# Two expert weight tiles per layer beside the ring, and a first pass of the expert loop written out

## The reference

```python
x += mixer(rmsnorm(x))        # layer 0: dilated sliding-window attention, layer 1: latent attention
x += hier_moe(rmsnorm(x))
x += (p[i] @ W_ple) * sigmoid(rmsnorm(x) @ W_ple_gate)
```

## Time and profile before

| | us |
|---|---|
| median of 3 runs | 1383.76 |
| lowest, highest | 1382.33, 1385.93 |
| profiled execution | 1388.38 |
| its span, first to last instruction | 1386.5 |

### The profile page before, as it was taken

How to read it: one execution, slowest core, us unless ns; L and a number is a source line. 1 busy time by engine, 2 the same in 40 slices (tenths; PEclk the granted TensorE clock), 3 DMA queues, 4 the chain that set the end, 5 groups by cost and what they waited for, 6 DMA issues and landing times.

```text
span 1386.5 us, 31096 instructions
## 1 busy us (share of the span) xinstructions
PE 1059.5 (76%) x13804; PEld 824.0 (59%) x13804; DVE 455.1 (33%) x1019; ACT 294.6 (21%) x567; POOL 9.3 (1%) x19
## 2 busy tenths in 40 slices
PE   6999999988666666666667989986666766765667
PEld 6999999865444545453445756564454444544446
DVE  6545555552112111111113675521121211111127
ACT  5433444221000000000003654210000000000017
POOL 1000000000000000000000000000000000000000
PEclk9999999999787998988898999998887888789888
DMA  9986540689999999999999740499999999999980
GB/s 275 313 235 173 159 123 0 260 370 425 426 426 426 426 426 426 425 427 425 426 427 385 307 173 1 182 428 425 429 424 426 428 424 426 428 423 425 427 347 32
DMA packets 114671, 470.02 MB, mean 339 GB/s; under 512 B 4689, under 2 KB 79569, under 8 KB 89841
## 3 DMA queue, kind: packets, MB, share of 16 engines
q1 hardware_dynamic: 113856, 465.78, 83.9%
q0 software_dynamic: 688, 2.28, 0.4%
HBM read 467.00 MB, written 1.05 MB: 338 GB/s over the span
## 4 chain that ended last, share of the span: by engine, by line
DMA 51%; PE 42%; DVE 3%; issue 2%; ACT 2%; DVEq 0%; SPq 0%; ACTq 0%
DMA ring<-moe_w_down 29%; DMA ring<-moe_w_up 11%; DMA ring<-moe_w_gate 11%; PE ps L1697 6%; PE ps L1468 5%; PE ps L1469 5%; PE ps L1470 5%; PE ps L1712 4%; PE ps L1582 2%; PE ps L1742 2%; PE ps L1784 1%; PE ps L1532 1%; PE ps L1508 1%; PE ps L1603 1%; PE ps L1875 1%
## 5 line engine op out<-in xcount | busy, mean ns | idle before, releaser
L1697 PE MATMUL ps<-ring,scr 128*32 128x128 f32 x8192 | 285.9, 300 | 154.3 <-DMA ring<-moe_w_up 98.7
L1697 PEld LDWEIGHTS ps<-ring,scr 128*32 128x32 f32 x8192 | 249.5, 120 | 192.8 <-DMA ring<-moe_w_up 109.2
L1712 PE MATMUL ps<-ring,scr 128*32 128x256 f32 x2048 | 175.3, 497 | 119.5 <-DMA ring<-moe_w_down 104.3
L1712 PEld LDWEIGHTS ps<-ring,scr 128*32 128x32 f32 x2048 | 83.8, 136 | 190.1 <-issue 118.4
L1188 DVE TENSOR_TENSOR scr<-scr,ps 128x128 f32<-128x128 f32 x64 | 23.8, 371 | 435.3 <-PE ps L1697 435.3
L728 ACT COPY scr<-ps 32x256 f32<-32x256 f32 x128 | 46.6, 364 | 552.7 <-PE ps L1712 551.9
L1201 DVE COPY scr<-ps 32x256 f32<-32x256 f32 x128 | 53.3, 417 | 248.7 <-PE ps L1712 247.8
L1468 PE MATMUL ps<-hT_hi,w_qk_hi 128*128 128x256 f32 x368 | 104.4, 284 | 0.0
L1470 PE MATMUL ps<-hT_hi,w_qk_lo 128*128 128x256 f32 x368 | 103.7, 282 | 0.0
L1469 PE MATMUL ps<-hT_lo,w_qk_hi 128*128 128x256 f32 x368 | 103.6, 282 | 0.0
L1603 PEld LDWEIGHTS ps<-scr,hs 128*128 128x128 f32 x512 | 66.3, 210 | 19.2 <-issue 19.2
(11 more groups left out here) (258 smaller groups left out, 1186.7 us busy)
## 6 DMA issues: line engine op xcount, KB each, us to landing
ring<-moe_w_gate SPq DMA_DIRECT2D x64, 2048.0 KB, 36.2
ring<-moe_w_up SPq DMA_DIRECT2D x64, 2048.0 KB, 36.6
ring<-moe_w_down SPq DMA_DIRECT2D x64, 2048.0 KB, 36.5
ring<-dsa_w_in SPq DMA_DIRECT2D x72, 512.0 KB, 6.7
ring<-ple_w_gate SPq DMA_DIRECT2D x4, 2048.0 KB, 37.0
ring<-dsa_w_out SPq DMA_DIRECT2D x2, 2048.0 KB, 13.9
ring<-mla_w_out SPq DMA_DIRECT2D x2, 2048.0 KB, 21.7
x_sb<-ple_w SPq DMA_DIRECT2D x2, 1024.0 KB, 7.1
```

What stands on the lines that cost most here:

```text
L1697: mm = pe.matmul(bank(b)[CW * q:CW * q + CW, 0:P], xT[:, k, :], tile(t + j, KD, FF)[:, k, P * q:P * q + P], start=(k == 0), stop=(k == KD ...
L1712: mm = pe.matmul(bank(6)[CW * q:CW * q + CW, 0:T], e_hT[:, CW * j:CW * j + CW], tile(t + 2, FF // P, D)[:, j, T * q:T * q + T], start=(j = ...
```

## The change

For each layer the down matrices of expert 0 and expert 1 (tiles 2 and 5 of the layer's order, `ASIDE`) leave the ring's numbering. They are kept in scratch, each in three pieces: two of its four row blocks together (1024 KB), and the other two alone (512 KB each), at places where `e_xT[1]` with `e_y`, `p_w`, `e_oneh` with what follows it, `f_gain` and `e_wt` will be later. SP issues three of the six pieces when the attention's last output product is done (`o_ready` in layer 0, `m_o_ready` in layer 1), before the ring tile that waits for the third `mix_out`, and the other three after the fourth `mix_out`. The eight tiles ahead of `ple_w` are then those numbered 0, 1, 3, 4, 6, 7, 8 and 9, and the loop on SP begins at tile 14. In layer 1 `f_gain` is loaded only after the second expert's down product, because its place holds a piece. The junk outputs of the squares get one buffer for both chunks, with a wait for the engine's own first square. On PE the first of the four passes is written out by a helper `expert(it, i)` with constants, whose down product for the first two experts reads the pieces, and the loop has three passes.

```diff
+ASIDE = (2, 5)
+SETTLED = RING + 6
+LOOPED = SETTLED + 3 * BODY * (ITERS - 1)
...
-    PLE = [MOE[0] + 3 * NE, 0]
+    PLE = [MOE[0] + 3 * NE - len(ASIDE), 0]
...
+        aside = [[scratch(3328, 2, D), scratch(9224, 1, D), scratch(10248, 1, D)],
+                 [scratch(256, 2, D), scratch(11272, 1, D), scratch(6528, 1, D)]]
...
-        junk_d, junk_a = [scratch(1024 * c, 512) for c in range(TC)], [scratch(1024 * c + 512, 512) for c in range(TC)]
+        junk_d, junk_a = scratch(2304, 512), scratch(2816, 512)
...
+            def load_aside(l, a, piece, rows):
+
+                e = ASIDE[a] // 3
+                sp.dma_start(aside[a][piece], moe_w_down[l, e:e + 1, :, :].rearrange("e (p j) n -> p (e j) n", p=P)[:, rows, :]
+                             ).then_inc(S(f"aside_{a}_in"), 16)
+
             def load_experts(l):
-                for n in range(RING):
+                ring_first = [n for n in range(SETTLED) if n not in ASIDE]
+                early, late = ring_first[:4 if l == 0 else 6], ring_first[4 if l == 0 else 6:RING]
+                for n in early:
+                    load_expert_tile(l, n)
+                if l == 0:
+                    sp.wait_ge(S("o_ready"), HEADS)
+                else:
+                    sp.wait_ge(S("m_o_ready"), MH // 2)
+                load_aside(l, 0, 0, slice(0, 2))
+                load_aside(l, 1, 0, slice(0, 2))
+                if l == 0:
+                    load_aside(l, 0, 1, slice(2, 3))
+                else:
+                    load_aside(l, 1, 2, slice(3, 4))
+                load_expert_tile(l, late[0])
+                sp.wait_ge(S("mix_out"), 4 * (l + 1))
+                if l == 1:
+                    load_aside(l, 0, 1, slice(2, 3))
+                load_aside(l, 0, 2, slice(3, 4))
+                load_expert_tile(l, late[1])
+                load_aside(l, 1, 1, slice(2, 3))
+                if l == 0:
+                    load_aside(l, 1, 2, slice(3, 4))
+                for n in late[2:]:
                     load_expert_tile(l, n)
 
                 sp.wait_ge(S("scattered"), (NGRP + 1) * l + 1)
                 sp.dma_start(x_sb[:, :, :], ple_w[l].rearrange("(k p) n -> p k n", p=P)).then_inc(S("p_in"), 16)
+                for n in ring_first[RING:]:
+                    load_expert_tile(l, n)
                 with sp.Fori(0, ITERS - 1) as it:
-                    for n in range(RING, RING + 3 * BODY):
+                    for n in range(SETTLED, SETTLED + 3 * BODY):
                         load_expert_tile(l, n, it)
...
                 if l == 1:
+                    pool.wait_ge(S("down_ready"), NE + ASIDE[1] // 3 + 1)
                     pool.dma_start(f_gain, rows[0:1, 2 * NR:2 * NR + D].partition_broadcast(P)
...
+                if i in (0, 1, 4) and c > 0:
+                    dve.wait_ge(S("sq_d"), TC * i + c)
...
-                with pe.Fori(0, ITERS) as it:
...
+                def wait_weights(it, i, j):
+
+                    if isinstance(it, int):
+                        t = Tiles.expert(l, 3 * i + j)
+                        wait_tile(pe, t)
+                    else:
+                        t = Tiles.expert(l, 3 * BODY + 3 * i + j)
+                        wait_tile(pe, t, (3 * BODY // RING) * (it - 1))
+                    return t
...
+                    if first and 3 * i + 2 in ASIDE:
+                        a = ASIDE.index(3 * i + 2)
+                        pe.wait_ge(S(f"aside_{a}_in"), 48 * (l + 1))
+                        down = [aside[a][0][:, 0, :], aside[a][0][:, 1, :], aside[a][1][:, 0, :], aside[a][2][:, 0, :]]
+                    else:
+                        t = wait_weights(it, i, 2)
+                        down = [tile(t, FF // P, D)[:, j, :] for j in range(FF // P)]
...
+                for i in range(BODY):
+                    expert(0, i)
+                with pe.Fori(1, ITERS) as it:
                     for i in range(BODY):
...
+                        expert(it, i)
```

More of the change, by code:

```diff
@@ L88, with expert, number @@
     MOE[1] = MLA_OUT + 2
-    PLE[1] = MOE[1] + 3 * NE
+    PLE[1] = MOE[1] + 3 * NE - len(ASIDE)
     N = PLE[1] + 2
+    @staticmethod
+    def expert(l, n):
+        assert n not in ASIDE
+        return Tiles.MOE[l] + n - sum(a < n for a in ASIDE)
+    @staticmethod
+    def number(l, t):
+        n = t - Tiles.MOE[l]
+        for a in ASIDE:
+            n += a <= n
+        return n
     @staticmethod
@@ L122, in used @@
         if t < Tiles.PLE[l]:
-            n = t - Tiles.MOE[l]
+            n = Tiles.number(l, t)
             return ("gate_ready", "up_ready", "down_ready")[n % 3], NE * l + n // 3 + 1
@@ L461, in load_expert_tile @@
             def load_expert_tile(l, n, it=0):
-                t, j = Tiles.MOE[l] + n, n % 3
+                t, j = Tiles.expert(l, n), n % 3
                 wait_free(t, BODY * it)
@@ new lines, in wait_weights, with expert @@
+                def wait_weights(it, i, j):
[6 more added lines that the diff above has]
+                    return t
+                def expert(it, i):
+                    first = isinstance(it, int)
+                    e = NE * l + BODY * it + i
+                    grp = (BODY // GE) * it + i // GE
+                    xT = e_xT[(i // GE) % 2][:, :, CW * (i % GE):CW * (i % GE) + CW]
+                    if i % GE == 0:
+                        pe.wait_ge(S("xT_ready"), xt0 + 2 * grp + 2)
+                    for j, b in ((0, 4), (1, 5)):
+                        t = wait_weights(it, i, j)
+                        for k in range(KD):
+                            for q in range(4):
+                                mm = pe.matmul(bank(b)[CW * q:CW * q + CW, 0:P], xT[:, k, :],
+                                               tile(t, KD, FF)[:, k, P * q:P * q + P],
+                                               start=(k == 0), stop=(k == KD - 1))
+                        mm.then_inc(S("gate_ready" if j == 0 else "up_ready"), 1)
+                    if i % GE == GE - 1:
+                        pe.wait_ge(S("wt_ready"), NGRP * l + grp + 1)
+                        pe.wait_ge(S("xT_ready"), xt0 + 2 * grp + 4)
+                        for c in range(TC):
+                            mm = pe.transpose(bank(7)[:, c * P:(c + 1) * P], e_wt[0][:, c, :], ident)
+                        mm.then_inc(S("wt_turned"), 1)
+                    pe.wait_ge(S("hT_ready_e"), e + 1)
+                    if first and 3 * i + 2 in ASIDE:
[5 more added lines that the diff above has]
+                        down = [tile(t, FF // P, D)[:, j, :] for j in range(FF // P)]
+                    for j in range(FF // P):
+                        for q in range(4):
+                            mm = pe.matmul(bank(6)[CW * q:CW * q + CW, 0:T], e_hT[:, CW * j:CW * j + CW],
+                                           down[j][:, T * q:T * q + T],
+                                           start=(j == 0), stop=(j == FF // P - 1))
+                    mm.then_inc(S("down_ready"), 1)
+                    if i == 1:
+                        pe.wait_ge(S("flag_ready"), l + 1)
+                    if i == GE:
+                        pe.wait_ge(S("pT_in"), 16 * (l + 1))
+                        pe.wait_ge(S("p_in"), 16 * (l + 1))
+                        for c in range(TC):
+                            for k in range(PLE // P):
+                                mm = pe.matmul(bank(7)[:, T * c:T * c + T], e_pT[:, k, c * P:(c + 1) * P],
+                                               x_sb[:, k, bass.ds(T * it, T)], start=(k == 0),
+                                               stop=(k == PLE // P - 1))
+                        mm.then_inc(S("pw_ready"), 1)
+                    if i == GE + 1:
+                        pe.wait_ge(S("pw_copied"), ITERS * l + it + 1)
+                    if i % GE in (1, 2):
+                        pe.wait_ge(S("oneh_ready"), TC * (NGRP * l + grp + 1))
+                        pe.wait_ge(S("xT_ready"), xt0 + 2 * grp + 2 + (i % GE - 1))
+                        gather(l, grp + 1, i % GE - 1)
+                    pe.wait_ge(S("y_copied_d"), e + 1)
+                    pe.wait_ge(S("y_copied_a"), e + 1)
+                    if i % GE == GE - 1:
+                        pe.wait_ge(S("sc_ready"), NGRP * l + grp + 1)
+                        for c in range(TC):
+                            for n in range(2):
+                                mm = pe.matmul(bank(2 * c + n), e_sc[:, c * P:(c + 1) * P],
+                                               e_y[:, 512 * n:512 * n + 512], start=False, stop=True,
+                                               skip_group_check=True)
+                            mm.then_inc(S("scattered" if c == TC - 1 else "scattered_0"), 1)
```

65 lines of the change are left out of this document (5 added, 60 removed).

## The result

The changed kernel takes 1366.63 us (median of 4 runs, 1364.75 to 1367.59). The kernel before, on the same chip, takes 1383.05 (4 runs). The ratio is 0.9864, 95% [0.9841, 0.9886]: on the 1383.76 of the prediction that is 18.8 us gained, between 15.8 and 22.0. The forecast was 14.6 gained, so 1369.2, with the range 1366.5 to 1373; the ratio puts the kernel at 1364.9, a little under the range. The two medians of this chip differ by less, 16.4 us, and the interval holds both; the same pair, timed again on another chip in experiment 6, gave 0.9868.

The account below looks back on a forecast made before the run. The prediction took DMA of expert weights at 425 GB/s to bound both loops. Layer 0's 6.0 us and layer 1's 8.6 made 14.6 gained, off the median 1383.76: 1369.2, own range 1366.5 to 1373, widened to 1366 to 1376.

Parts of the forecast that it names:

- the first pass written out: PE's expert loop, one jump back fewer per layer: value 0, bounds 5.75 us gained and up to 2.5 lost per written pass.
- it shifts whole: Between the expert loops and after the second, the change touches nothing on the chain, so no time is gained or lost.
- What bounds the kernel: Both expert loops: DMA of weight tiles at 425 GB/s sets the end; PE's pace inside the loop costs nothing.
- Layer 0's term: Layer 0's expert stream: 6.17 us gained by early pieces less 0.2 for short rows, 6.0 us in all.
- 6.17 us of stream are gained: Layer 0: three early pieces, 2.62 MB, fit into idle DMA time before the sixth tile, with about 1 us to spare.
- The term for short rows: Layer 0's pieces come in 8 and 4 KB rows, not 16 KB: 0.2 us lost, bounds 0 and 0.4.
- Layer 1's term: Layer 1's expert stream: 9.87 us gained by all six pieces less 1.3 for the later `f_gain`, 8.6 us in all.
- The same 152 us: Sign: the stretch from layer 0's last tile to layer 1's `ple_w` keeps its length of 152 us.
- rival (a): Half the gain: layer 1's routing slowed beside transfers, layer 0 possibly clipped; 6 to 8 us left, 1376.5; chance 0.12.
- (b): PE's code waits at the loops' pass changes are on the path: 14.6 + 11.5 us gained, 1357.7; chance 0.04.
- (d): Pieces don't queue into one another, 4.9 us each in the DMA queue: 10.4 us slower, 1394.2; chance 0.05.
- (c): Gain given back whole because PE, not DMA, ends the expert loop: 1383.8; chance 0.03.

Follow-up runs that it names:

- experiment 6: The changed kernel, unchanged, timed again on another chip: 1367.44 us, ratio 0.9868 to the kernel before.
- experiment 7: The changed kernel with the `f_gain` broadcast done four times, one after the other: 1372.42 us, ratio 0.9886 to the kernel before.
- experiment 1: The kernel before with only PE's first pass written out, no tiles beside the ring: 1379.82 us, ratio 0.9944.
- experiment 10: The changed kernel with both PE loop heads set at instruction 29 of a 16 KB code piece: 1367.74 us, ratio 0.986 to the kernel before.
- experiment 3: The changed kernel with PE's loop heads set at instructions 57 and 77 of a 16 KB code piece: 1372.1 us, ratio 0.9907 to the kernel before.
- experiment 2: The kernel before with 170 semaphore increments on PE around the first transposes of `x`, shifting later code: 1392.53 us, ratio 1.0058.
- 12: The kernel before, unchanged, run once more for a second profile: 1386.35 us, ratio 0.9995.
- experiment 9: The changed kernel with each piece beside the ring loaded by four issues in 1 KB rows: 1367.79 us, ratio 0.9862 to the kernel before.
- experiments 4: The changed kernel with tiles beside the ring in layer 1 alone: 1371.07 us, ratio 0.9889 to the kernel before.
- experiment 5: The changed kernel with tiles beside the ring in layer 0 alone: 1376.13 us, ratio 0.9921 to the kernel before.

## Why the prediction was wrong, and what of it held

The terms of the two tiles held. What failed is the step that put everything outside the two streams at nothing: the first pass written out at "Value 0", and "Between the loops and after the second nothing in the change touches the chain [...], so it shifts whole". Written out alone, the pass measured 7.7 us. With the routing that is told below, 14.0 of stream + 7.7 − 1.6 = 20.1, inside the measured 15.8 to 22.0.

**What bounds the kernel** held. The plateaus stay at 425 to 426 GB/s in every kernel of the study, and layers without the tiles take 491.9 to 494.1 and 445.1 to 446.1 us, with them 487.1 to 488.5 and 436.3 to 437.1 (the four `f_gain` of experiment 7 left out). The means of the two sets are 4.9 and 9.1 apart, 14.0 against 14.6 forecast.

**Layer 0's term** was 6.0 and is 4.9 (4.6 in the first pair of traces). The step that mis-sized it is "6.17 us of stream are gained": it asked whether the bytes fit and never summed the hole. In 4 us windows from 272 to 296, what lacks to 425 GB/s is 2.1, 0.4 and 3.2 us and, from a later look at the same trace, 1.3 and then nothing, about 7.0 in all. After it is 0.1, 0.1, 0.0, 1.2, 0.2 and 0.4, about 2.0. The gain is the difference, 5.0. The hole from 284 to 288, while the sixth tile's queue starts, is in both kernels. The term for short rows, 0.2, doesn't look like what is missing: with rows of 1 KB the stream is as long. The mean hides one more thing. Routing of layer 0 comes in a short and a long form (last section), and without the tiles the long one leaves a hole of its own: in experiment 1 the stream has 305 and 379 GB/s from 300 to 308, where before has 408 and 428. The streams without tiles are 491.9 to 492.2 with the short form and 493.4 and 494.1 with the long one; with tiles they are 487.1 to 488.5 with either. So the tiles are worth 4.5 or 5.9 in layer 0, by the form.

**Layer 1's term** was 8.6, with 1.3 off for `f_gain`; the stream gave 9.1 (9.6 in the first pair of traces). The pieces fit as forecast and no large hole opened behind `ple_w`. The three extra `f_gain` at 1.2 each confirm the price of an added one, the 0.2 for taking the only one away does not; both cannot be the whole story, and this stays open.

**The first pass written out, at value 0,** was wrong: 7.7 us, [0.9925, 0.9964]. The argument looked at the pass changes inside the loop, which indeed stay free. After, PE still waits 2.83 and 4.85 us at one of layer 1 and 3.02 us in the next expert, in a full stream:

```profile
1093.18 0.66 PE L1763 MATMUL ps<-ring,scr 128*32 128x128 f32 x8 [2.83 <-issue]
1098.69 5.69 PE L1763 MATMUL ps<-ring,scr 128*32 128x128 f32 x120 [4.85 <-issue]
...
1114.42 1.86 PE L1763 MATMUL ps<-ring,scr 128*32 128x128 f32 x26 [3.02 <-issue]
```

The upper bound, 5.75 for a pass change in each layer, was on the wrong waits. The sentence behind the sum, that nothing outside the loops is touched, is where it failed: writing out a pass puts some 2800 more PE instructions ahead of each loop's exit (2788 by the count in the expectation of experiment 10), and so the exit and what follows fall elsewhere within the pieces in which PE's code arrives. The rows for it stood in the trace of before, at 754.58 and 1351.37, at a place that I did not read because no edit touches it.

The pieces can be counted in the trace: q8, the instruction queue, moved 1.85 MB in 113 packets before, 16.4 KB each, and 110 packets after. A loop's place in them can be read as well. After a jump back, PE's second wait comes 112 matmul records in with the head set at 29, 98 with 57, 88 with 77 and 51 with 152: the count and half the position always make 126.5 or 127. The 97 of before in layer 0 and its 89 in layer 1 then belong to heads at 59 and 75 or so, within two instructions of those that experiment 3 set.

The Trainium skill, "Runtime: NRT & Kernel Launch", section "Instruction fetch mechanics", has code arrive in 16 KiB blocks of 256 instructions, with which the packets and the counts here agree. The Trainium skill calls the cost of crossing a block's end mostly hidden there; if the 3.39 us on the path at 754.58 are such a crossing, they differ, and the measurement decides. What the prediction made of the Trainium skill's advice to unroll, 11.5 us more, gives 26.1 in all, further from the measured 18.8 than the forecast's 14.6, and not for the reason seen here: experiment 2 unrolls nothing and loses the waits as well.

What is shown is that the waits come and go with the position of the code (experiments 1, 2, 3, 12), and that their going was worth 7.7 us in experiment 1. That a piece is fetched too late is a reading of these rows; none shows the fetch itself waiting, and no rule of position came out that fits all of them. For layer 1 the wait was never put back.

**The routing of layer 1.** "The same 152 us" for the stretch between the loops hid three terms: −5.0 from the gate stage with the wait in it, −1.9 from the attention, and +1.6 from routing. Of the attention's 1.9, some 1.2 look like clock: before runs at 0.59 from 876 to 880, and its second trace has no such window there and is 1.2 shorter. From POOL's iota to `ple_w` it takes 13.84 us in before and 15.46 after. That was rival (a)'s place, but not by its cause: the slower form is there in the kernel with tiles in layer 0 alone (15.47), and the faster one in experiment 9 with tiles in both (13.83). The +1.6 is in experiments 4 and 5 alike, against experiment 1: with it off, layer 1's 9.1 of stream become 7.5 (7.6 measured) and layer 0's 4.9 become 3.3 (3.2 measured). In the changed kernel it comes once, so the sum of three parts in experiment 5 takes it off twice.

**Rivals.** (b), code waits on the path, had 0.04 and the sum 14.6 + 11.5. It was half right: code waits are on the path, but at the loops' ends and for 7.7, not at the pass changes. (d) is refuted: from 272 to 284, with three pieces of 0.5 to 1 MB in a row in the queue, DMA runs at 410 to 420 GB/s. (c) did not occur. Of the signs named, pieces issued at 268, no valley from 272 to 284 and plateaus at 425 came; layer 0's last tile landed at 740.17 for the 738 named. What was named for layer 1 came earlier, since all before it is earlier: its pieces at 855.43 for 865, the last tile at 1323.41 for 1328; `ple_w` of layer 1 came 146.82 after layer 0's last tile, where I had named over 152.3 as the sign of failure and had no sign for less.

## What to carry to other kernels

A gain from earlier loads is the hole in the stream before minus the hole after, summed window by window, not the bytes that fit in. Before an edit that changes the length of an engine's code is put at nothing, look in the whole trace for idle time put down to "issue", above all where a loop ends and DMA no longer covers it: such an edit can remove or make one, here 2.4 to 3.6 us each, and 3.2 to 4.0 in the mean of the stage with what the clock adds. Don't read the price of such a wait from one pair of traces: without any code wait the same stages varied by 3 to 4 us with the granted clock. When two builds differ by less than 1%, a third in which nothing but the code's place is changed tells how much of that is position; put the padding where it costs no time.

## What the runs showed of the hardware

Layer 1's routing, from POOL's iota to `ple_w`, takes one of two lengths and nothing between: 13.81 to 13.84 or 15.46 to 15.47 us over 14 profiled executions; layer 0's 12.80 to 12.81 or 15.46 to 15.48. In layer 0 of the changed kernel the granted clock is 0.50 from 288 to 292, with PE busy 4.00 of 4 us (window above); in before it is 1.00 there. The length goes with that clock and not with the tiles: it is 12.80 in experiment 3 and 15.47 in experiment 6, which differ only in where the loop's head stands. In layer 0 the queue hides it where the tiles stand beside the ring, and not where they don't; in layer 1 it is on the path. Which edit brings which is open.

Semaphore increments are not free at the start of a kernel: 170 of them on PE delayed the first expert tile by 12.3 us, 0.07 each at the least, since PE had idle time there before.
